# The score products of head pairs over 64 rows instead of 128, in a two-block model kernel

## The reference

```python
HEAD_DIM = 64
# diff: 4 heads x 2 maps of 64; q and k with partial rope
s = jnp.einsum('bhcqd,bhckd->bhcqk', q[:, :, :, q0:q1], k[:, :, :, :q1]).astype(jnp.float32) * scale
# stick-breaking, 8 heads of 64
z = jnp.einsum('bhqd,bhkd->bhqk', q[:, :, q0:q1], k[:, :, :q1]).astype(jnp.float32) * scale
# forgetting, 8 heads of 64
logits = jnp.einsum('bhqd,bhkd->bhqk', q[:, :, q0:q1], k[:, :, :q1]).astype(jnp.float32) * scale
logits = logits + cum_log_f[:, :, q0:q1, None] - cum_log_f[:, :, None, :q1]
```

## Time and profile before

| | |
|---|---|
| median of 3 runs | 1962.1 us |
| the profiled execution | 1963.62 us, span 1961.8 us |
| mean granted TensorE clock | 0.992 of 2.4 GHz |
| TensorE products | busy 1889.1 us, 96% |
| weight loads (PEld) | 1539.6 us, 78% |
| ScalarE | 876.9 us, 45% |
| VectorE | 778.7 us, 40% |
| GpSimd | 662.5 us, 34% |

### The profile page before, as it was taken

The page is one execution under the profiler, slowest core; times in us unless marked ns, Lnnn a source line. Parts: engine busy times, 40 slices in busy tenths (PEclk is TensorE's granted clock), DMA queues, the critical chain, the costliest instruction groups (busy, mean ns, idle before and its releaser), DMA issues.

```text
span 1961.8 us, 24062 instructions
## 1 busy us (share of the span) xinstructions
PE 1889.1 (96%) x9239; PEld 1539.6 (78%) x9239; DVE 778.7 (40%) x1346; ACT 876.9 (45%) x1727; POOL 662.5 (34%) x278
## 2 busy tenths in 40 slices
PE   8999999899999999989999999999999999999998
PEld 6887787777788788777777888888788878888886
DVE  3435656446434565645545842111350441111002
ACT  4556565554445555555435632333453352233222
POOL 2432333213242133322233543443104424443442
PEclk9999999999999999999999999999999999999999
DMA  4321222213332222211332232322102422322232
GB/s 155 108 65 57 84 86 78 63 54 114 116 104 65 67 74 86 77 64 54 108 139 69 97 98 91 97 86 89 41 1 97 140 76 97 97 97 97 97 97 86
DMA packets 48412, 170.06 MB, mean 87 GB/s; under 512 B 6961, under 2 KB 7217, under 8 KB 47665
## 3 DMA queue, kind: packets, MB, share of 16 engines
q1 hardware_dynamic: 46480, 154.95, 24.2%
q10 hardware_dynamic: 1824, 13.63, 1.8%
HBM read 155.97 MB, written 6.29 MB: 83 GB/s over the span
## 4 chain that ended last, share of the span: by engine, by line
PE 83%; DVE 9%; ACT 4%; issue 3%; DMA 0%; POOL 0%; DVEq 0%; ACTq 0%; POOLq 0%
PE bank L670 13%; PE bank L672 13%; PE bank L671 13%; PE bank L673 10%; PE bank L675 10%; PE bank L674 10%; PE bank L797 3%; PE bank L814 2%; PE bank L775 1%; PE bank L773 1%; PE bank L776 1%; DVE y_tok L1423 1%; PE bank L828 1%; PE bank L761 1%; PE bank L827 1%
## 5 line engine op out<-in xcount | busy, mean ns | idle before, releaser
L653 POOL TENSOR_TENSOR w_hl<-w_raw,w_hl 128x1024 fp32r<-128x1024 f32 x274 | 662.3, 2421 | 1275.2 <-ACT w_hl L925 1274.7
L925 ACT ACTIVATE w_hl<-w_raw 128x1024 fp32r<-128x1024 f32 x274 | 287.6, 1058 | 346.6 <-DMA w_raw<-wstream 346.0
L670 PE MATMUL bank<-act_hl,w_hl 128*128 128x512 f32 x1056 | 426.5, 404 | 3.1 <-DVE act_hl L1296 1.9
L672 PE MATMUL bank<-act_hl,w_hl 128*128 128x512 f32 x1056 | 413.9, 392 | 0.0
L671 PE MATMUL bank<-act_hl,w_hl 128*128 128x512 f32 x1056 | 413.3, 391 | 0.0
L673 PE MATMUL bank<-w_hl,act_hl 128*128 128x512 f32 x672 | 265.6, 395 | 4.4 <-POOL w_hl L653 2.0
L675 PE MATMUL bank<-w_hl,act_hl 128*128 128x512 f32 x672 | 262.6, 391 | 0.0
L674 PE MATMUL bank<-w_hl,act_hl 128*128 128x512 f32 x672 | 262.3, 390 | 0.0
L670 PEld LDWEIGHTS bank<-act_hl,w_hl 128*128 128x128 f32 x1056 | 200.1, 189 | 44.9 <-issue 3.9
L672 PEld LDWEIGHTS bank<-act_hl,w_hl 128*128 128x128 f32 x1056 | 199.4, 189 | 43.2
L671 PEld LDWEIGHTS bank<-act_hl,w_hl 128*128 128x128 f32 x1056 | 200.1, 189 | 40.8 <-issue 2.2
(11 more groups left out here) (231 smaller groups left out, 2800.7 us busy)
## 6 DMA issues: line engine op xcount, KB each, us to landing
w_raw<-wstream SPq DMA_DIRECT2D x274, 512.0 KB, 3.5
q_dup<-q_dup SPq DMA_DIRECT2D x48, 128.0 KB, 3.7
x_spill<-x_res ACTq DMA_DIRECT2D x2, 2048.0 KB, 7.0
x_res<-x_spill ACTq DMA_DIRECT2D x2, 2048.0 KB, 8.0
x_res<-x SPq DMA_DIRECT2D x4, 512.0 KB, 5.8
g_post<-post_gains ACTq DMA_DIRECT2D x4, 512.0 KB, 3.8
x_res<-x ACTq DMA_DIRECT2D x1, 2048.0 KB, 8.1
out<-x_res SPq DMA_DIRECT2D x4, 512.0 KB, 2.6
```

Of the source, the lines that this page charges most:

```text
L653: nc.gpsimd.tensor_tensor(w_hl[:, slot, 1].rearrange("p c n -> p (c n)"), w_raw[:, slot, :], w_hl[:, slot, 0].rearrange("p c n -> p (c n)" ...
L670: pe.matmul(out_ap, wh, ah, start=start, stop=False)
L672: return pe.matmul(out_ap, wl, ah, start=False, stop=stop)
L925: nc.scalar.activation(w_hl[:, b % RING, 0].rearrange("p c n -> p (c n)"), w_raw[:, b % RING, :], ACT.Copy).then_inc(s_high_done, 1)
```

## The change

Queries and keys are kept as they are projected: `q_hl[:, p, 0]` is the high part of both heads' queries in all 128 rows and `q_hl[:, p, 1]` the low part; `k_hl` is laid out in the same way. `pair_scores` computes both heads of a unit together: for each of the three combinations of parts it issues one product over rows 0 to 63 into head 0's bank and one over rows 64 to 127 into head 1's. The ck product of the fox kind and the masks stay as they were, per head, behind the six. Each bank of q or k is split by one instruction of 128 rows on ScalarE and one on VectorE. `q_twice`, its semaphores, `q_dup`, `q_low` and the memsets go.

```diff
--- before.py
+++ after.py
@@ -333,10 +333,9 @@
     y_acc = at("y_acc", [P, TT, D], f32)
     vv = at("vv", [P, TT, 4 * P], f32, over)
     gate = at("gate", [P, 4, S], f32)
-    q_dup = at("q_dup", [P, 4, 2, S], f32r)
+    q_hl = at("q_hl", [P, 4, 2, S], f32r)
     y_fox = at("y_fox", [P, 4, 2, S], f32r, cursor[0] - 4 * 2 * S * 4)
     raw_fox = at("raw_fox", [P, 4, 2, S], f32, cursor[0] - 4 * 2 * S * 4)
-    q_low = at("q_low", [P, 4, 2, S], f32r)
     k_hl = at("k_hl", [P, 4, 2, S], f32r)
     sel_r = at("sel_r", [P, 8], f32r)
     ck = at("ck", [P, S], f32r)
@@ -401,7 +400,6 @@
     s_rows_max = nc.alloc_semaphore("rows_max")
     s_sticks = nc.alloc_semaphore("sticks")
     s_qk_high = nc.alloc_semaphore("qk_high")
-    s_q_twice = [nc.alloc_semaphore(f"q_twice{m}") for m in range(2)]
     s_v_high = nc.alloc_semaphore("v_high")
     s_p_high = nc.alloc_semaphore("p_high")
     s_soft = nc.alloc_semaphore("soft")
@@ -591,7 +589,6 @@
             return
         for done_tile in (group_turned if kind == "diff" else group_drained)(group("qk", l=l, kind=kind, m=m)):
             pe.wait_ge(*done_tile)
-        pe.wait_ge(s_q_twice[m], 4 * 16 * (len(KINDS) * l + KINDS.index(kind) + 1))
         if kind == "fox":
             pe.wait_ge(s_ck_ready, l + 1)
 
@@ -624,22 +621,9 @@
                     for dst, src in CONSTS:
                         sp.dma_start(whole(dst), whole(src)).then_inc(s_consts, 16)
                 sp.dma_start(w_raw[:, b, :], wstream[b]).then_inc(loaded[b], 16)
-            def q_twice(g):
-
-                for j in (0, 2):
-                    p = 2 * g["m"] + j // 2
-                    sp.wait_ge(s_qk_high, MARKS["qk_high", (g["index"], j)])
-                    for a in range(2):
-                        own, other = slice(a * HD, (a + 1) * HD), slice((1 - a) * HD, (2 - a) * HD)
-                        sp.dma_start(q_dup[other, p, a, :].bitcast(f32), q_dup[own, p, a, :].bitcast(f32))\
-                            .then_inc(s_q_twice[g["m"]], 16)
-
-            twice = {g["first"] + g["n"] - 1 + (1 if g["kind"] == "diff" else 0): g for g in GROUPS if g["tag"] == "qk"}
             for b in range(RING, NB):
                 sp.wait_ge(s_block_used, b - RING + 1)
                 sp.dma_start(w_raw[:, b % RING, :], wstream[b]).then_inc(loaded[b % RING], 16)
-                if b - RING in twice:
-                    q_twice(twice[b - RING])
             for t in range(TT):
                 sp.wait_ge(s_x_new, 3 * TT + t + 1)
                 sp.dma_start(out.rearrange("b (t p) d -> p (b t) d", p=P)[:, t, :], x_res[:, t, :]).then_inc(s_stored, 16)
@@ -761,19 +745,27 @@
                         tr = pe.transpose(to[:, t * P:(t + 1) * P], tok_tmp[:, t, j * P:(j + 1) * P], ident[:, :])
                     tr.then_inc(filled(("rope", gi, j)), 1)
 
+            def pair_scores(l, kind, n, p, rows, keys):
+
+                for q_part, k_part in ((0, 0), (0, 1), (1, 0)):
+                    for a, half in enumerate((slice(0, HD), slice(HD, P))):
+                        pe.matmul(bank_of(("S", l, kind, n, a))[:, keys], q_hl[half, p, q_part, rows],
+                                  k_hl[half, p, k_part, keys], start=(q_part == k_part), stop=False)
+
             def scores(l, kind, n):
                 p, i = n // 4, row_tile(kind, n)
+                rows = slice(i * P, (i + 1) * P)
+                for a in unit_maps(kind):
+                    if earlier(("S", l, kind, n, a))[1] > 0:
+                        pe.wait_ge(*earlier(("S", l, kind, n, a)))
+                if kind != "dil":
+                    pair_scores(l, kind, n, p, rows, slice(0, (i + 1) * P))
                 for a in unit_maps(kind):
                     first, nb = geometry(kind, a, i)
-                    if earlier(("S", l, kind, n, a))[1] > 0:
-                        pe.wait_ge(*earlier(("S", l, kind, n, a)))
                     to = bank_of(("S", l, kind, n, a))
-                    rows, keys = slice(i * P, (i + 1) * P), slice(first * P, (first + nb) * P)
+                    keys = slice(first * P, (first + nb) * P)
                     if kind == "dil":
                         pe.matmul(to[:, 0:nb * P], q2[:, a * H2 + p, rows], k2[:, a * H2 + p, keys], start=True, stop=False)
-                    else:
-                        pe.matmul(to[:, 0:nb * P], q_dup[:, p, a, rows], k_hl[:, p, a, keys], start=True, stop=False)
-                        pe.matmul(to[:, 0:nb * P], q_low[:, p, a, rows], k_hl[:, p, a, keys], start=False, stop=False)
                     if kind == "fox":
 
                         pe.matmul(to[:, 0:nb * P], sel_r[:, 2 * p + a:2 * p + a + 1].broadcast_to([P, P]), ck[:, 0:nb * P],
@@ -1030,16 +1022,13 @@
 
             def qk_high(g, j, ps):
 
-                p, heads_ = 2 * g["m"] + j // 2, (slice(0, HD), slice(HD, P))
+                p = 2 * g["m"] + j // 2
                 if j % 2 == 0:
                     if (g["l"], g["ki"]) != (0, 0):
                         act.wait_ge(*full(("S",) + prev_kind(g["l"], g["kind"]) + (4 * p + 3, 1)))
-                    for a in range(2):
-                        ins = nc.scalar.activation(q_dup[heads_[a], p, a, :], ps[heads_[a], :], ACT.Copy, scale=HD ** -0.5)
+                    nc.scalar.activation(q_hl[:, p, 0, :], ps[:, :], ACT.Copy, scale=HD ** -0.5).then_inc(s_qk_high, 1)
                 else:
-                    for a in range(2):
-                        ins = nc.scalar.activation(k_hl[heads_[a], p, a, :], ps[heads_[a], :], ACT.Copy)
-                ins.then_inc(s_qk_high, 1)
+                    nc.scalar.activation(k_hl[:, p, 0, :], ps[:, :], ACT.Copy).then_inc(s_qk_high, 1)
 
             def rope(gi):
                 g = GROUPS[gi]
@@ -1275,8 +1264,6 @@
                 link(nc.vector.tensor_copy(sel_r[:, :], sel[:, :]))
                 for l in range(DEPTH):
                     link(nc.vector.tensor_scalar(sub_g[:, l:l + 1], sub_g[:, l:l + 1], 1.0 - LAM_INIT[l], None, ALU.mult))
-                for a, rows in enumerate((slice(HD, P), slice(0, HD))):
-                    link(nc.vector.memset(q_low[rows, :, a, :].bitcast(f32), 0.0))
 
             def norm_row(i, t):
 
@@ -1385,18 +1372,16 @@
 
             def qk_low(g, j, key):
 
-                p, heads_ = 2 * g["m"] + j // 2, (slice(0, HD), slice(HD, P))
+                p = 2 * g["m"] + j // 2
                 dve.wait_ge(s_qk_high, MARKS["qk_high", (g["index"], j)])
                 ps = bank_of(key)
-                for a, rows in enumerate(heads_):
-                    if j % 2 == 0:
-                        ins = nc.vector.scalar_tensor_tensor(
-                            out=q_low[rows, p, a, :], in0=ps[rows, :], scalar=HD ** -0.5,
-                            in1=q_dup[rows, p, a, :].bitcast(f32), op0=ALU.mult, op1=ALU.subtract)
-                    else:
-                        ins = nc.vector.tensor_tensor(k_hl[heads_[1 - a], p, a, :], ps[rows, :],
-                                                      k_hl[rows, p, a, :].bitcast(f32), ALU.subtract)
-                ins.then_inc(freed(key), 1)
+                if j % 2 == 0:
+                    nc.vector.scalar_tensor_tensor(
+                        out=q_hl[:, p, 1, :], in0=ps[:, :], scalar=HD ** -0.5, in1=q_hl[:, p, 0, :].bitcast(f32),
+                        op0=ALU.mult, op1=ALU.subtract).then_inc(freed(key), 1)
+                else:
+                    nc.vector.tensor_tensor(k_hl[:, p, 1, :], ps[:, :], k_hl[:, p, 0, :].bitcast(f32), ALU.subtract)\
+                        .then_inc(freed(key), 1)
 
             def rope_low(gi):
```

## The result

The changed kernel takes 1967.43 us, median of 12 runs (1965.85 to 1969.59), beside 1963.32 for the kernel before (12 runs on the same chips). The ratio is 1.0025, with a 95% interval of 1.0017 to 1.0032: slower, by just over what can be told from no change. The forecast was 1940.4, faster, with a range of 1931 to 1972: the time lies in that range, among the prices of the rivals, and the direction is the other one.

The account below looks back on a forecast made before the run. TensorE, busy 96% of the span, was taken as the bound. -16.2 - 7.0 - 4.1 - 3.5 + 7.1 + 2.0 = -21.7 on 1963.6 gives 1941.9, 1940.4 as median; range 1931 to 1972.

Parts of the forecast that it names:

- splits and copies: Whole-bank q and k splits: shorter fox stall -7.0, lower clock -4.1, q_low waits -3.5; removed q copies 0.
- joint wait of the pairs: Score products: both heads' banks must be free first, +7.1 over 14 units, and +2.0 for the later first head's scores.
- score products: TensorE's score products: three side-by-side pairs replace four products, -19.2, less 3 lost to longer waits: -16.2 us.
- dil kind: Dilated attention of the second block: the forecast named no wait or cost there.
- Change of shape: Array going from 128-row to 64-row products and back each unit, 192 changes: taken as 0 from the forget products.
- rival of the emptying array: Array empties at each shape change, 0.16 each: +31, 1971; without loading weights ahead 9 more, 1980; chance 0.12.
- wait for pt_hl: Fox kind's second pair of q and k: pt_hl split ends at 383.4 instead of 386.9, 3.5 us a layer, -7.0.
- the 3 that the forecast had set aside for waits: Taken off the score products' -19.2, where TensorE waits for other engines' chains and the saving becomes a longer wait.
- the wait that comes in: Before each unit's first score product, both heads' banks must be free: 14 units at 0.3 to 0.6, +7.1, and +2.0.
- The stall: TensorE's wait of 4.51 before L797 in the fox kind: should be near 1, without a lower clock behind it.
- q_low waits: TensorE's four waits for a q_low split before refilling a bank, 3.5 in total: bank free 1.2 us earlier, -3.5.
- the 4.1 of lower clock behind the stall: Behind the fox stall the clock falls to 1.2 GHz, costing 2.6 and 1.5 us in two layers: -4.1 expected.

Follow-up runs that it names:

- splits and copies alone: Changed kernel's layout and whole-bank splits, two 128-row products a head instead of pairs, waits as before; scores not the reference's: 1943.75 us, 0.9897 to the kernel before.
- the joint wait added: As splits and copies alone, but both heads' banks must be free before the first product, except in the dil kind: 1948.79 us, 0.9927 to the kernel before.
- the waits put back: Changed kernel, but in the dil kind each map waits for its own bank again: 1954.53 us, 0.9957 to the kernel before.
- moved in the kernel before: Kernel before, with only the dil kind's three waits moved ahead of all products of a unit: 1974.14 us beside 1962.25, ratio 1.0061.
- Six full products: As the waits put back, but each of the six score products runs over all 128 rows: 1972.15 us, 1.0040 to the kernel before.
- the heads apart: As the waits put back, but head 0's three 64-row products precede head 1's, each head with its own wait: 1953.74 us, 0.9960 to the kernel before.

## Why the prediction was wrong, step by step

| step | predicted | measured | by |
|---|---|---|---|
| splits and copies | -14.6 | -20.2 | splits and copies alone, against before |
| joint wait of the pairs | +9.1 | +5.0 | the joint wait added |
| score products | -16.2 | +5.7 | the pairs for four full products |
| dil kind | nothing | +13.5, and +11.9 by itself | the waits put back, and moved in the kernel before |

Measured, the four sum to the result, +4.1 (4.0 by the rounded terms); they must, since each step starts where another ends. The +13.5 is taken between two distances from the kernel before, +4.1 and -9.4, because the two kernels didn't run on the same chips. The run of the dil kind's waits by itself, +11.9, is the term that could have come out otherwise.

**Change of shape: this step failed.** "I take 0", it says, on the strength of the forget products with 40 weight columns. A change in the number of weight columns is free in the earlier trace rows, and in the trace after as well (16 forget products in 45.06 - 41.34 = 3.72 us), but going between 128-row and 64-row products costs 0.19 us on the way in and 0.10 on the way out, 0.29 a unit and 28 us over 96 units. That is the rival of the emptying array, to which I had given 0.12, and in size a little under its lower end of 31. It isn't quite the rival's mechanism, though. The rival let a product start only when the record of the last one had ended, 0.16 a change; measured, the two gaps are 0.09 and 0.10, and the other 0.10 is the late load of the second pair's weights, which the rival had as its higher end. The Trainium skill (TensorEngine Tiling (Array Packing), Key Properties) says that changing the tiling mode drains the TensorE. By that rule the trace after agrees, with 0.10 coming out, and 0.09 + 0.10 going in; the rows I held against it were of another kind of change.

**Score products: mis-sized by 21.9 for that reason** (28, less the 3.5 that the shorter wait for pt_hl gives back, 14.1 to 10.6, and less the 3 that the forecast had set aside for waits, is 21.5). The mechanism of the pairs was right: two run in the time of one, and so do their weight loads, since the second and third pair of 128 columns stand 0.11 apart and not 0.22. Before the prices the unit would have saved 0.31 at 512 keys and 0.10 at 128; with 0.29 against it, it saves nothing at 512 and loses 0.17 at 128. In the fox kind, where the masks can't stand together, the units lose up to 0.19. Six full products are 17.6 us slower than the pairs, so side by side is worth something; it isn't worth two changes of shape in place of one product of at most 512 columns.

**The dil kind: missed.** The section on the change shows the loop of waits ahead of `if kind != "dil"`, and the prediction has a part on the wait that comes in, but I followed it only through the three kinds that the change is about. A fourth kind goes through the same function, with three banks and no dense products between its units to hide a wait. It took 12 to 13.5 us, of which waits are 9.4 and the lower clock behind them 1.7, and is what turned a gain into a loss: without it the changed kernel would be at 1954.5, faster than before by 0.4%, still above the forecast because of the changes of shape.

**The joint wait: the mechanism right, the size too big.** The wait grew from 5.0 to 10.6, as told (about 12); +9.1 should have been +5.0. With nothing but the joint wait added, the wait in the list grew by 4.7, and in 10 places; the forecast had counted 14 units at 0.5 and 0.15 more in each for the longer chain. Why the others cost nothing wasn't looked at.

**Splits and copies: right, and too small.** The stall went from 4.51 to 0.56 (told: near 1), without a lower clock behind it, and the q_low waits are gone. Of the 20.2, three parts stand in the lists as forecast: the wait for pt_hl is down by 21.3 - 14.2 = 7.1, the 3.5 for q_low are gone, and so are the 4.1 of lower clock behind the stall. One part was overlooked. In the kernel before, the clock also falls behind the wait of 1.56 at the end of the first diff kind; in the profile of the splits alone the same wait is there, 1.59, and the clock stays. The windows of the two, the kernel before first:

```profile
177.00:181.00 4.00, 3.58 (x16) 3.27 (x17) 2.13 (x7) 1.56 (x6) 0.00 (x0) 0.57 0.02 4
...
176.00:181.00 5.00, 3.66 (x22) 3.18 (x23) 3.38 (x10) 2.60 (x11) 0.00 (x0) 1.00 0.02 5
```

That is (1 - 0.57) x 4 = 1.7 us, and it may be chance: in the changed kernel the clock falls there again. The remaining 3.8 stay open, and with them whether the copies that went were worth something.

## What to carry to other kernels

When a line of waits is moved in a function that several callers share, go through every caller, the untouched stages first: a wait that names several banks at once gives up the overlap of the first bank's work with the freeing of the last. Products over half of the rows have to earn the change of shape: here one in and out costs 0.29 us, more than one product of 512 columns (0.23), so three pairs that save one such product gained nothing between full-row products. Whether longer stretches in the 64-row shape pay wasn't tried. And what relieves the engines beside TensorE can be worth more than what relieves TensorE: the whole-bank splits, with the copies gone, gave 20 us, and 11 of them by shortening one chain on ScalarE and VectorE that TensorE waited for once a layer, with the lower clock behind it.

## What the runs showed of the hardware

Two halves of the array work through their own products independently. With three products on rows 0 to 63 ahead of three on rows 64 to 127 in the program, the six took 0.97 us from first start to last end, as when they alternate; one after the other would be 1.15 + 0.39 = 1.54, and six full products are 1.52. The Trainium skill (TensorE: Matmul & The Clock Gate, Part 3) says that matmuls keep the program's order in start and end; the heads apart don't bear that out between two halves.

Two masks in bf16 behind each other share one late fp32r load: behind them the dense product's record is 0.48 as it was behind one.
